# Expert rooms refilled by rows, last transfers by column halves, and constant products in TensorE's waits

## What is computed

```python
def rms_norm(x, w):
    xf = x.astype(jnp.float32)
    y = xf * lax.rsqrt(jnp.mean(xf * xf, axis=-1, keepdims=True) + EPS)
    return (y * w.astype(jnp.float32)).astype(x.dtype)

# first layer, start:   h = rms_norm(x, norm1_w);  u = h @ w_in
# first layer, middle:  top_k of the index scores picks the keys, then softmax attention on them
# second layer, end:
def expert_choice_ffn(u, w_router, w_gate, w_up, w_down):
    cap = CAPACITY_FACTOR * l // N_EXPERTS                     # 32 tokens an expert
    logits = jnp.einsum('bld,de->ble', u, w_router).astype(jnp.float32)
    aff = jax.nn.softmax(logits, axis=-1)
    g, idx = lax.top_k(aff.transpose(0, 2, 1), cap)
    ...
```

## Time and profile before

| what | value |
|---|---|
| median of three runs | 1196.36 us |
| the profiled execution | 1196.45 us |
| its span | 1194.5 us |
| TensorE busy | 92% of the span |
| VectorE, ScalarE busy | 42%, 35% |
| read from memory | 307.5 MB |
| mean granted clock of TensorE | 0.983 |

### The profile page before, as it was taken

The page is one execution under the profiler, slowest core; times in us unless marked ns, Lnnn a source line. Parts: engine busy times, 40 slices in busy tenths (PEclk is TensorE's granted clock), DMA queues, the critical chain, the costliest instruction groups (busy, mean ns, idle before and its releaser), DMA issues.

```text
span 1194.5 us, 16626 instructions
## 1 busy us (share of the span) xinstructions
PE 1098.5 (92%) x6691; PEld 785.0 (66%) x6691; DVE 507.0 (42%) x999; ACT 419.2 (35%) x800; POOL 16.4 (1%) x28
## 2 busy tenths in 40 slices
PE   7999999999999999999999996998978797879786
PEld 6988988888999999798678885332323232323231
DVE  4778774795666555676875323010101000100011
ACT  4667666844666444664345312000100000000000
POOL 3000000000000000000000000000000000000000
PEclk9999999999999999999999997999999999999998
DMA  8735334343465667254241985799999999999995
GB/s 230 247 116 190 116 130 145 128 157 135 148 211 157 176 163 208 83 199 141 72 141 72 361 333 221 295 427 427 428 427 427 429 427 428 427 428 430 424 422 235
DMA packets 95108, 309.45 MB, mean 259 GB/s; under 512 B 6016, under 2 KB 41096, under 8 KB 83080
## 3 DMA queue, kind: packets, MB, share of 16 engines
q1 hardware_dynamic: 94296, 307.42, 66.8%
q0 software_dynamic: 496, 1.07, 0.4%
q10 hardware_dynamic: 256, 0.10, 0.0%
HBM read 307.53 MB, written 1.05 MB: 258 GB/s over the span
## 4 chain that ended last, share of the span: by engine, by line
PE 72%; DMA 23%; DVE 3%; ACT 1%; issue 1%; SPq 1%; ACTq 0%; DVEq 0%
PE bank L438 71%; DMA parts_room<-in_w_up 7%; DMA arena<-in_w_down 4%; DMA parts_room<-in_w_down 3%; DMA arena<-in_w_up 3%; DMA ring<-in_w_down 3%; DMA xh<-in_w_down 2%; SPq L1137 1%; PE bank L671 0%; DMA arena<-in_x 0%; DVE parts L1689 0%; DVE roots_room L1661 0%; DVE hidden_parts L1901 0%; DVE arena L2218 0%; ACT parts L1262 0%
## 5 line engine op out<-in xcount | busy, mean ns | idle before, releaser
L438 PE MATMUL bank<-parts 128*128 128x256 f32 (+1 forms) x2352 | 299.8, 288 | 1.4 <-issue 1.2
L438 PEld LDWEIGHTS bank<-parts 128*128 128x128 f32 x2352 | 288.3, 191 | 15.2 <-issue 12.0
L1262 ACT ACTIVATE parts<-ring 128x512 fp32r<-128x512 f32 x328 | 203.7, 629 | 227.1 <-PE bank L438 218.2
L1689 DVE TENSOR_TENSOR parts<-ring,parts 128x512 fp32r<-128x512 f32 x328 | 218.9, 689 | 120.5 <-ACT parts L1262 118.7
L438 PE MATMUL bank<-hidden_parts,parts 128*128 128x256 f32 x1024 | 164.9, 283 | 0.0
L438 PE MATMUL bank<-arena 128*32 128x512 f32 (+4 forms) x548 | 149.7, 487 | 11.3 <-DMA arena<-in_w_down 2.7
L438 PE MATMUL bank<-arena,roots_room 128*32 128x512 f32 x400 | 131.6, 607 | 15.4 <-DMA ring<-in_w_gate 5.5
L438 PEld LDWEIGHTS bank<-hidden_parts,parts 128*128 128x128 f32 x1024 | 141.4, 192 | 0.1
L2205 DVE TENSOR_TENSOR sqr<-bank,arena 128x512 f32<-128x512 f32 x8 | 5.2, 686 | 273.5 <-ACT arena L1579 273.5
L438 PEld LDWEIGHTS bank<-arena 128*128 128x128 f32 (+2 forms) x548 | 78.8, 194 | 54.1 <-issue 40.8
L438 PE MATMUL bank<-ring,roots_room 128*32 128x512 f32 x224 | 98.2, 600 | 7.8 <-DMA xh<-in_w_up 4.0
(11 more groups left out here) (300 smaller groups left out, 955.3 us busy)
## 6 DMA issues: line engine op xcount, KB each, us to landing
ring<-in_w_in SPq DMA_DIRECT2D x21, 2048.0 KB, 8.0
arena<-in_w_gate SPq DMA_DIRECT2D x14, 2048.0 KB, 34.6
arena<-in_w_down SPq DMA_DIRECT2D x13, 2048.0 KB, 37.1
arena<-in_w_up SPq DMA_DIRECT2D x11, 2048.0 KB, 36.8
ring<-in_w_ff_in SPq DMA_DIRECT2D x8, 2048.0 KB, 7.8
ring<-in_w_ff_out SPq DMA_DIRECT2D x8, 2048.0 KB, 9.0
parts_room<-in_w_up SPq DMA_DIRECT2D x8, 2048.0 KB, 36.8
ring<-in_w_gate SPq DMA_DIRECT2D x7, 2048.0 KB, 35.3
```

Of the source, the lines that this page charges most:

```text
L438: return nc.tensor.matmul(o, lhsT=l, rhs=r, start=first, stop=last)
L1262: A(w_part[0][:, p % PIECES], piece_of(n, p), ACT.Copy).then_inc(S("pieces rounded"), 1)
L1689: X.tensor_tensor(w_part[1][:, p % PIECES], piece_of(n, p), w_part[0][:, p % PIECES].bitcast(F32), ALU.subtract).then_inc(S("pieces split" ...
```

## The change

What it does, by place:

1. **Start.** GpSimd first writes zeros into 256 columns of `sqr`. TensorE waits for them and does 13 products of zeros by zeros with 256 columns (`keep_clock`) ahead of the norm vector's turn. x is scaled into `xnormed` by ScalarE and VectorE (two copies of 512 columns each), and is then turned with the identity. All four `turn_x` come first.
2. **Middle.** `att_scores(a)` waits for the pads of its own pair of heads only. ScalarE writes the fourth pair of pads ahead of the rounding that it followed. VectorE forms the rest of a half after six selection rounds instead of after eight.
3. **Router.** 7, 11, 1 and 2 products of the identity with the 512-column `iota` tile, into a bank that is free, stand in the order of TensorE's work around the turns and the gather.
4. **First refill.** The first expert block of the first group works on all four experts by rows j. After each row, SP loads that row of units 10 to 13 into the rooms (16 transfers of 512 KB in place of four of 2 MB).
5. **Last transfers.** The last four units go out as eight transfers of 1 MB, each a row j and one half of the columns: first the four rows of the lower half, then the four of the upper. The lower half is copied, and its sums formed, before the upper half is done. In the other groups too ScalarE copies the lower half as soon as it is summed.
6. **Between the last transfers** stand 22 more constant products: 5 ahead of the lower half's pieces, 6 after its second, 1 after its last, 3 ahead of the upper half's, and 1, 2, 3 and 1 after its four pieces.

```diff
+            def keep_clock(n, b, stationary, moving):
+                for _ in range(n):
+                    mm(bank[b][:, 0:moving.shape[1]], stationary, moving)
+            pe.wait_ge(S("filler set"), 1)
+            keep_clock(13, 3, sqr[:, 0, 0:P], sqr[:, 0, 0:T])
             pe.wait_ge(S("identity loaded"), 16)
...
-            turn_x(0)
-            turn_x(1)
+            for b in range(4):
+                turn_x(b)
             for b in range(4):
                 ps = take(b, ("h", b))
                 for t in range(TT):
-                    if b == 0:
-                        pe.wait_ge(S(f"x {t} scaled"), 1)
+                    if b % 2 == 0:
+                        pe.wait_ge(S(f"x {t} scaled"), b // 2 + 1)
                     for k in (2 * b, 2 * b + 1):
                         c = (k % 2) * T + t * P
-                        last = mm(ps[:, c:c + P], xtok[:, t, k * P:k * P + P], xdiag[:, t, :])
+                        last = nc.tensor.transpose(ps[:, c:c + P], xnormed[:, t, k * P:k * P + P], ident)
...
-                pe.wait_ge(S("keys padded"), 8)
+                pe.wait_ge(S("keys padded"), 2 * g + 2)
...
             route_tiles(3)
+            free_bank = (turn + 1) % 4
+            keep_clock(7, free_bank, ident, C("iota"))
             pe.wait_ge(S("affinity"), 2)
...
+            keep_clock(11, free_bank, ident, C("iota"))
             pe.wait_ge(S("ranked"), 1)
...
+            keep_clock(1, free_bank, ident, C("iota"))
...
             gather(6, slice(0, P))
+            keep_clock(2, free_bank, ident, C("iota"))
...
+                def first_block_by_rows():
+                    for e in range(GROUP):
+                        unit_ready(e)
+                    for j in range(RUN):
+                        for h in range(2):
+                            last = product(0, range(GROUP), 0, xg, 0, h, j)
+                        if j < RUN - 1:
+                            last.then_inc(S("expert row"), 1)
+                        else:
+                            last.then_inc(S("expert block"), GROUP // PAIR)
...
+                def last_pieces(h):
+                    for j in range(RUN):
+                        n = LAST_ROWS + (RUN * h + j) // 2
+                        if h == 1 and j == 2:
+                            pe.wait_ge(S("last piece but one loaded"), 16)
+                        else:
+                            pe.wait_ge(moe_loaded[n % MOE_RING], 16 * (n // MOE_RING + (1 if h and j == 3 else 2)))
+                        for e in range(GROUP):
+                            last = mm(bank[4 + h][CAP * e:CAP * e + CAP, :],
+                                      hhT[:, KD - RUN + j, CAP * e:CAP * e + CAP], last_piece(RUN * h + j)[:, e, :],
+                                      False, j == RUN - 1)
+                        if j == RUN - 1:
+                            last.then_inc(S("expert block" if h else "lower half summed"), 1)
+                        elif h == 0 and j == 1:
+                            last.then_inc(S("expert block"), 1)
+                            keep_clock(6, 7, ident, C("iota"))
+                        elif h:
+                            keep_clock(1 + j, 7, ident, C("iota"))
+                    keep_clock(1, 7, ident, C("iota"))
                 for h in range(2):
+                    if last_group:
+                        keep_clock(3 if h else 5, 7, ident, C("iota"))
+                        last_pieces(h)
...
+            def refill_by_rows():
+                for j in range(RUN):
+                    if j < RUN - 1:
+                        sp.wait_ge(S("expert row"), j + 1)
+                    else:
+                        sp.wait_ge(S("expert block"), GROUP // PAIR)
+                    for n in by_rows:
+                        v, e = n // (2 * RUN), n % RUN
+                        rows_of = I[("w_gate_2", "w_up_2")[(n // RUN) % 2]][0, e, P * RUN * v:P * RUN * (v + 1), :].rearrange("(p j) c -> p j c", j=RUN)
+                        sp.dma_start(moe_slot(n)[:, 0, j, :], rows_of[:, j, :])\
+                            .then_inc(S("rows refilled") if j < RUN - 1 else moe_loaded[n % MOE_RING], 16)
...
-                    sp.dma_start(moe_room[n % MOE_RING].rearrange("p (e c) -> p e c", c=D), rows_of[:, n - LAST_ROWS])\
-                        .then_inc(moe_loaded[n % MOE_RING], 16)
+                    for i in (2 * (n - LAST_ROWS), 2 * (n - LAST_ROWS) + 1):
+                        h, j = i // RUN, i % RUN
+                        sp.dma_start(last_piece(i), rows_of[:, j, :, 512 * h:512 * h + 512])\
+                            .then_inc(S("last piece but one loaded") if i == 2 * RUN - 2 else moe_loaded[n % MOE_RING], 16)
...
-            A(xdiag[:, 0, :], ident, ACT.Copy, scale=xscale[:, 0:1]).then_inc(S("x 0 scaled"), 1)
+            for h in range(2):
+                A(xnormed[:, 0, 512 * h:512 * h + 512], xtok[:, 0, 512 * h:512 * h + 512], ACT.Copy, scale=xscale[:, 0:1])\
+                    .then_inc(S("x 0 scaled"), 1)
...
-            round_half(EARLY)
             pad_keys(3)
+            round_half(EARLY)
...
-                act.wait_ge(S("expert block"), g * BLOCKS + BLOCKS)
+                act.wait_ge(S("lower half summed"), g + 1)
...
-            select_rounds(0, range(0, 8))
+            select_rounds(0, range(0, 6))
+            rest_of_half(7)
+            select_rounds(0, range(6, 8))
             key_bias(0)
-            rest_of_half(7)
...
+            G.memset(sqr[:, 0, 0:T], 0.0).then_inc(S("filler set"), 1)
+            G.memset(eps, EPS).then_inc(S("constants set"), 1)
```

More of the change, by code:

```diff
@@ L225, in two_layers @@
         xsquared = area(4128, 2, D)
-        xdiag = area(6176, 2, P)
+        xnormed = area(6176, 2, D)
         rnn = area(0, 8, T + 4)
@@ L345, in two_layers, with last_piece @@
         moe_loaded = [S(f"expert ring slot {s} loaded") for s in range(MOE_RING)]
+        by_rows = range(MOE_RING, MOE_RING + GROUP)
+        def last_piece(i):
+            room = moe_room[(LAST_ROWS + i // 2) % MOE_RING]
+            return room[:, UNIT // 2 * (i % 2):UNIT // 2 * (i % 2 + 1)].rearrange("p (e c) -> p e c", c=512)
         def moe_slot(n):
@@ L989, in unit_ready @@
                     n = first_unit + u
+                    if n in by_rows:
+                        pe.wait_ge(S("rows refilled"), 16 * len(by_rows) * (RUN - 1))
                     pe.wait_ge(moe_loaded[n % MOE_RING], 16 * (n // MOE_RING + 1))
@@ L995, in experts, with product, block @@
                     pe.wait_ge(emptied[b], g * 2 + ug[b])
-                def block(u, pair, banks, src, q):
+                def product(u, pair, banks, src, q, h, j):
+                    k = RUN * q + j
+                    for e in pair:
+                        w = moe_slot(first_unit + u + e)[:, 0, j, 512 * h:512 * h + 512]
+                        last = mm(bank[banks + h][CAP * e:CAP * e + CAP, :], src[:, k, CAP * e:CAP * e + CAP], w,
+                                  k == 0, k == KD - 1)
+                    return last
+                def block(u, pair, banks, src, q, lower=""):
                     for i in pair:
@@ L1001, in block @@
                         for j in range(RUN):
[L1002 to L1006, removed]
-                    last.then_inc(S("expert block"), 1)
-                block(0, (0, 1), 0, xg, 0)
-                block(0, (2, 3), 0, xg, 0)
+                            last = product(u, pair, banks, src, q, h, j)
+                        if h == 0 and lower:
+                            last.then_inc(S(lower), 1)
+                    last.then_inc(S("expert block"), 1)
+                def first_block_by_rows():
[8 more added lines that the diff above has]
+                            last.then_inc(S("expert block"), GROUP // PAIR)
+                if g:
+                    block(0, (0, 1), 0, xg, 0)
+                    block(0, (2, 3), 0, xg, 0)
+                else:
+                    first_block_by_rows()
                 pe.wait_ge(emptied[7], g + ug[7])
@@ L1038, in experts @@
                     if not (last_group and q):
-                        for pair in ((0, 1), (2, 3)):
-                            block(2 * KD + RUN * q, pair, 4, hhT, q)
-                if last_group:
+                        block(2 * KD + RUN * q, (0, 1), 4, hhT, q)
+                        block(2 * KD + RUN * q, (2, 3), 4, hhT, q, "lower half summed" if q else "")
+                def last_pieces(h):
                     for j in range(RUN):
[L1043 to L1050, removed]
+                        n = LAST_ROWS + (RUN * h + j) // 2
[10 more added lines that the diff above has]
+                        elif h == 0 and j == 1:
                             last.then_inc(S("expert block"), 1)
+                            keep_clock(6, 7, ident, C("iota"))
+                        elif h:
+                            keep_clock(1 + j, 7, ident, C("iota"))
+                    keep_clock(1, 7, ident, C("iota"))
```

(13 more changed lines are left out.)

9 lines of the change are left out of this document (5 added, 4 removed).

## The result

The kernel after takes **1219.79 us**, the median of four runs (1219.26 to 1220.28), beside 1196.39 (1196.31 to 1198.15) for the kernel before: a ratio of 1.0202, 95% interval 1.0189 to 1.0215 (ratios and intervals are estimates over the executions; the two medians alone give 1.0196, and in the runs below the two differ by up to 0.0013). The change costs 23.4 us. The direction was as forecast, and the size was nearly five times the forecast +4.95. The time lies outside the range of 1181 to 1205.

The account below looks back on a forecast made before the run. Bounds: when TensorE reaches the expert layer, when the refill restarts, and what follows the last landing. Terms -0.6 - 1.9 + 6.5 - 6.8 + 1.15 + 6.6 = +4.95 gave 1201.3 us by the median, range 1181 to 1205.

Parts of the forecast that it names:

- Rows -6.8: First expert block by rows: SP's first refill follows the block's start sooner than the 8.7 us before, -6.8 us.
- The head: Start: thirteen products delay VectorE, but scaling x before its turns lets the first dense products begin at 14.3, -0.6 us.
- Rival (2): Head: the clock rises late and TensorE finishes the thirteen products at 11.7; 1204.0 us, chance 0.14.
- The middle: Scores and selection: TensorE's waits of 1.60 and 0.65 go, 0.3 given back to VectorE, -1.9 us.
- The router: Constant products outlast TensorE's waits around turns and gather, so the first expert block starts later, +6.5 us.
- The row transfers: Refill by rows: transfers with 4 KB runs go at 405 GB/s instead of 429, +1.15 us.
- The upper bound: Row transfers: at most +3.9 us, backed by the skill's 341 GB/s for a lone 1 MB transfer.
- The tail: After the last landing: TensorE, late through 22 constant products, ends the last addition 16.6 us behind it, +6.6 us.
- The halves alone "would have brought it to L + 4.4": Tail: column halves and ScalarE's earlier copy alone would end the last addition 4.4 us after the last landing.
- L: Tail: the time of the last landing of a transfer; the last addition before the change ended 10.05 us after it.
- (1): All constant products fit in the waits: 1180.5 us at the one-pass price, 1183.9 at 0.43 a product; chance 0.26.
- Rival (4): Refill: 16 issues hold SP back, the rows do not free the queue, stream starves by 3.9 us; 1204.1, chance 0.05.

Follow-up runs that it names:

- a_order: Kernel after with one edit: SP's refill by rows moved ahead of the wait for the third expert block; 1204.77 us, ratio 1.0072 to the kernel before.
- h: Kernel before plus only the first expert block and refill by rows, refill ahead of the third block's wait; 1189.73 us, ratio 0.9945.
- k: Kernel before plus only the first expert block and refill by rows, refill behind the third block's wait; 1206.15 us, ratio 1.0101.
- b: Kernel after without any constant products, SP's order unchanged; 1200.46 us, ratio 1.0036 to the kernel before.
- c: Kernel after without any constant products and with the refill ahead of the third block's wait; 1184.93 us, ratio 0.9902 to the kernel before.
- j: Kernel before plus only the head's new order and the two changes of the middle, no constant products; 1191.72 us, ratio 0.9967.
- i: Kernel before plus only the last transfers by column halves and ScalarE's earlier copy, no constant products; 1192.61 us, ratio 0.9977.
- d: Kernel after with the refill ahead of the third block's wait and without the tail's 22 constant products; 1191.84 us, ratio 0.9961 to the kernel before.
- g: Kernel after with the refill ahead of the third block's wait and every constant product at half its columns; 1187.79 us, ratio 0.9939 to before.
- f: Kernel after with the refill moved ahead and only 4, 6, 0 and 1 constant products, in the router; 1183.99 us, ratio 0.9902 to before.

## Why the prediction was right and wrong

**The step that failed is "Rows -6.8".** It assumed that SP loads each row as soon as its products are done. The products and the waits inside `refill_by_rows` are as it said, but the call stands behind another wait in SP's list. What queued behind the third block's wait was the refill itself. It was +9.3 in place of -6.8. The reading of the diff was at fault, not a price: the wait stands two statements above the call that the change adds, in a branch whose condition it only narrows. `a_order` and the pair h and k show it: one moved call is 15.0 us between after and a, and 1.6% of the time between k and h; with the call moved the step measures 1.99 - 8.71 = -6.7.

**The head: -0.6, measured -0.8.** The thirteen products ended at 9.15 (forecast 9.0), VectorE's square of x began at 9.55 (9.4), the scaled turns at 12.27 (12.1) and the dense products at 14.05 (14.3), for 14.87 before. Part of the match is luck: the products began at 1.10 and not at 1.6, and took 8.05 and not 7.4. Rival (2), the late clock, did not come, but is not far: the same records took 8.54 in a, whose dense products began at 14.54. Without the products, the dense products began at 12.6, 12.2 and 12.0 (b, c, j), so the products cost the head 1.4 to 2.1 us.

**The middle: -1.9, right.** The 1.60 is gone. The 0.65 is gone from its place, and one of 0.46 stands 48 records later; `j_front` has 0.47 there without any constant product. The forecast had given back 0.3. Head and middle together are -2.7 (the row at 296.50 before starts at 293.84), for a forecast of -2.5.

**The router: +6.5, right.** Seven pairs of records took 6.26 (6.0), eleven 9.61 (9.4), VectorE's ranks were ready 4.0 before TensorE was (4.1), the gather kept its 3.93. The first block started at 749.56, and 745.84 - 2.5 + 6.5 is 749.84.

**The row transfers: +1.15, right in the runs that isolate it** (+1.2 in h and k), and hidden in the kernel after, whose chain to the end runs through TensorE's work and not through these transfers. The upper bound is out: a queue of 512 KB transfers moved 409 and 412 GB/s. The Trainium skill (DMA: Bandwidth & Descriptors, "Bandwidth") gives 341 GB/s for a transfer of 1 MB. The windows here don't agree with it for a backlog: 409 and 412 with 512 KB, and 388 with the last pieces of 1 MB. The estimate that the prediction drew from that page, 24.6 us for the rows, is also not what the bound says: it is 5.0 over the 19.6 of before, and 3.9 over the forecast's own 20.7.

**The tail: +6.6, too small by 2.3 and 1.0.** It was right that TensorE is late for the last landing and never waits after it. The work from the end of the last full block was put at 29.2 and took 1182.31 to 1213.80, 31.5. The term that the sum lacks is the change between kinds of product. From start to start a piece of eight records takes 1.00 (1201.20 to 1202.20) where the sum had 0.86, and the one constant product behind it 1.06 (1202.20 to 1203.26), again for 0.86. So a change costs 0.14 one way and 0.20 the other. Of each there are six in the tail: 2.0 of the 2.3. After the last addition another 1.05 was lost that the sum put at nothing. Its cause is open. SP issues the last store 0.02 to 0.03 after the last addition in every kernel here, so the loss lies behind that. Three of the four additions stand together now, and the stores with them, but that is not it: i has the same and ends 4.37 after its last addition, as before does, and j, with the additions of before, ends 5.42 after. d shows what the 22 products cost in all, 12.9 beside the same kernel without them; the forecast would have had 16.6 - 4.4 = 12.2.

**The halves alone "would have brought it to L + 4.4".** Measured in i: L + 4.6. But L itself is 0.8 later, for which no term stood, and the L + 10.05 it is held against has half clock in it: the same tail ends at L + 7.1 in j and k.

**The rivals.** (1) at 0.26: the rows of the router decide against it, a product is two records of 0.43. Its arithmetic, 1183.9 for products at 0.43, also assumed the early refill; g, which has both (0.45 a product), took 1187.79. Not on the list was the case that came: a queue that an edit is placed behind. Rival (4) stood next to it, "the rows do not free the queue", but for another reason and at 1204.1.

## What to carry to other kernels

For each instruction that a change adds to a queue, list what the queue passes directly before it, the untouched lines included: a wait that was harmless ahead of its old neighbour held 16 transfers for 16 us here. Work that only fills waits has to be counted in the engine's own records of the same type, since the sign here turned on 0.43 or 0.86 us for a product. And put to an early refill, a split last transfer and a shorter front their own runs: each was worth 0.2 to 0.6% here, and all three were hidden under the price of the constant products and one misplaced call.

## What the runs showed of the hardware

**Changing the kind of product costs time.** Alternating between products of 32 columns of weights, four side by side, and products of a full tile cost 0.14 us from the former to the latter and 0.20 back, by the starts in the tail of the kernel after. The same steps in a are 0.13 and 0.20, and in g, whose full-tile products are half as long, 0.14 and 0.15 to 0.18. No run changed this alone.

**A gather that the clock hardly helps.** The 16 products of the gather took 3.93 at a granted clock of 1.00 and 4.07 to 4.08 at 0.50 (after; b and c). The turns next to it gained more: 0.29 for 0.39, and 0.38 for 0.59. In the kernel after weight loads are busy for 4.32 of the 5 us from 744 to 749, which would fit loads that set the gather's pace; no run changed them.

**Rate by run of bytes, in a full queue.** 429 GB/s with 16 KB runs in transfers of 2 MB, 405 with 4 KB runs in 2 MB, 409 to 412 with 4 KB runs in 512 KB, and 388 with the 2 KB runs of the last pieces, in 1 MB. Between the middle two only the size differs, and it made little difference. The last is this window of the kernel after:

```profile
1176.00:1183.00 7.00, 7.00 (x32) 2.31 (x29) 0.00 (x0) 0.00 (x0) 0.00 (x0) 1.00 1.05 388
```

**The clock in the tail is not the same in like kernels.** b, c, d, f and i have no constant products there. Their last two sums (four records) took 3.57, 3.78, 3.53, 1.98 and 1.98 us, at half clock or nearly in the first three and at full in the others. From the start of the last piece's products to the end of the last addition that makes 6.2, 7.0, 6.1, 4.6 and 4.6, so up to 2.4 us of the whole time. The kernel before's own tail shows it too: 10.0, where h, j and k, with the same instructions there, have 8.8, 7.1 and 7.1. What decides it is not shown; each is one execution.
